# Differential attention on halves of the array's rows, with the second map read against the first half's minimum

## The reference, cut to what matters

```python
def diff_attention(q, k, v, lam, slopes):
    # q, k: (B,S,H,2,Dh), v: (B,S,H,2Dh); S = 2048, H = 4, Dh = 64
    def block(args):                       # 128 queries at a time
        qblk, qp = args
        s = jnp.einsum('bqhce,bkhce->bchqk', qblk, k).astype(jnp.float32) * Dh ** -0.5
        dist = jnp.abs(qp[:, None] - pos[None, :]).astype(jnp.float32)
        s = s - slopes[:, None, None] * dist
        a = jax.nn.softmax(s, axis=-1)
        w = a[:, 0] - lam * a[:, 1]
        return jnp.einsum('bhqk,bkhe->bqhe', w.astype(v.dtype), v)
    ...
a = diff_attention(dq, dk, dv, lam, diff_slopes)
a = rms_norm(a, diff_sub_norm_g[i]) * (1.0 - lam_init)
```

## Time and profile before

| what | value |
|---|---|
| time, median of 3 runs | 2989.01 us (2987.17 to 2992.03) |
| the profiled execution | 2989.96 us, its span 2988.1 us |
| TensorE, weight loads | busy 2801.3 us (94%), 2324.2 us (78%) |
| VectorE, ScalarE, GpSimd | busy 2049.3 (69%), 1554.8 (52%), 1027.6 us (34%) |
| granted TensorE clock, mean | 0.971 |
| the stage of the change | 762 to 1343 us of the span |

### The profile page before, as it was taken

One profiled execution on the slowest core, in us unless ns is written; L12 is line 12 of the kernel. 1 busy time (PEld: TensorE's weight loads), 2 busy tenths in 40 slices (PEclk: granted clock), 3 DMA queues, 4 the chain that ended last, 5 costly groups with the idle time before them and its releaser, 6 DMA issues. The chain is left out here.

```text
span 2988.1 us, 50265 instructions
## 1 busy us (share of the span) xinstructions
PE 2801.3 (94%) x19042; PEld 2324.2 (78%) x19042; DVE 2049.3 (69%) x3063; ACT 1554.8 (52%) x3111; POOL 1027.6 (34%) x736
## 2 busy tenths in 40 slices
PE   6899989999799999998999699899898999799998
PEld 5678867888588888888999578688777778677776
DVE  5766686665888888876777677433567777466675
ACT  6574446643677777766777322322343343355553
POOL 4667657766311111009652444200020111131121
PEclk9999999999899999999999899999999999899999
DMA  3433223333302120004443656342155456654441
GB/s 113 127 106 106 92 85 92 100 105 104 97 23 51 27 54 23 22 11 144 116 117 96 212 198 248 134 143 79 57 161 128 114 142 167 158 165 138 133 154 73
DMA packets 317421, 329.86 MB, mean 110 GB/s; under 512 B 24400, under 2 KB 259968, under 8 KB 314112
## 3 DMA queue, kind: packets, MB, share of 16 engines
q1 hardware_dynamic: 287184, 292.59, 32.1%
q0 software_dynamic: 6912, 23.07, 2.6%
q10 hardware_dynamic: 23088, 11.02, 1.6%
HBM read 217.13 MB, written 109.47 MB: 109 GB/s over the span
## 5 line engine op out<-in xcount | busy, mean ns | idle before, releaser
L1049 PE MATMUL p_acc<-p_y_hi,p_x_hi 128*128 128x512 f32 x904 | 361.7, 400 | 11.6 <-POOL p_x_lo L562 3.8
L1926 DVE CUSTOM_DVE_ANT_0 d_e<-d_score,d_dist,d_slope 128x1024 f32<-128x1024 f32 x256 | 318.5, 1281 | 59.4 <-PE d_score L1988 59.4
L1049 PE MATMUL p_acc<-p_y_lo,p_x_hi 128*128 128x512 f32 x904 | 355.9, 394 | 0.0
L1049 PE MATMUL p_acc<-p_y_hi,p_x_lo 128*128 128x512 f32 x904 | 355.6, 393 | 0.0
L562 POOL TENSOR_TENSOR p_x_lo<-k_carry,p_x_hi 128x1024 fp32r<-128x1024 f32 x113 | 281.1, 2494 | 130.7 <-ACT p_x_hi L634 130.7
L1853 ACT ACTIVATE d_e<-d_e,d_neg_top 128x2048 f32<-128x2048 f32 x128 | 257.0, 2008 | 81.7 <-DVE d_neg_top L1935 81.7
L920 DVE RECIPROCAL p_aux<-p_aux 128x512 f32<-128x512 f32 x64 | 215.1, 3361 | 57.8 <-ACT p_aux L730 57.8
L2011 PE MATMUL d_out<-d_v,d_w_t 128*128 128x128 f32 x2048 | 249.3, 275 | 0.0
L1565 PE MATMUL s_acc<-s_y_hi,s_x_hi 128*128 128x512 f32 x560 | 225.1, 402 | 23.8 <-DVE s_x_lo L1369 13.5
L2011 PEld LDWEIGHTS d_out<-d_v,d_w_t 128*128 128x128 f32 x2048 | 238.6, 192 | 0.0
L1565 PE MATMUL s_acc<-s_y_lo,s_x_hi 128*128 128x512 f32 x560 | 221.9, 396 | 0.0
(11 more groups left out here) (363 smaller groups left out, 6964.0 us busy)
## 6 DMA issues: line engine op xcount, KB each, us to landing
k_carry<-in_w_in SPq DMA_DIRECT2D x128, 256.0 KB, 3.3
k_carry<-in_a_w_in POOLq DMA_DIRECT2D x72, 256.0 KB, 3.6
cols<-p_z SPq DMA_DIRECT2D x64, 256.0 KB, 2.6
w_q<-q SPq DMA_DIRECT2D x15, 1024.0 KB, 8.0
o_parts<-l_stage SPq DMA_DIRECT2D x192, 66.0 KB, 1.8
m_o<-o_parts SPq DMA_DIRECT2D x48, 264.0 KB, 5.9
k_carry<-cols SPq DMA_DIRECT2D x48, 256.0 KB, 4.6
j_x_second<-x SPq DMA_DIRECT2D x20, 512.0 KB, 3.7
```

The lines of the kernel that those rows point to most:

```text
L1049: mm = pe.matmul(bank_of(n, j), x_part[:, n % RING, j, kt], y_part[:, y_slot(n), kt], start=(kt == 0 and m == 0 and not (g == 0 and n % 2 ...
L1926: dve.tensor_tensor_reduce(e[:, m % 3, s, half * HALF:(half + 1) * HALF], score[:, 2 * half:2 * half + 2].rearrange("p a b -> p (a b)"), d ...
```

## The change

`EARLY` is 3; `wait_mixed` waits for the half of the mix that belongs to the group, `wait_turn_free` for `moved` at 4m + 2 group, `wait_group_moved` at 4m + 2 group + 2. The transposes are made in two groups of eight key tiles. Each tile is turned by two instructions, one for the queries 0 to 63 and one for 64 to 127, each on 64 rows and each into its own bank of `turn`; so the two banks are full after one group. The values are two matmuls a tile, one for the keys on rows 0 to 63 and one for the others, into two banks of `out`, which are no longer doubled by unit. ScalarE copies both banks into `a_parts`, GpSimd adds them into `a_out`, ScalarE squares from there, and SyncE's store waits for the add. VectorE's second read of a map takes the first's minimum as its start and yields the whole map's; the reductions of L1935 are gone, and the signs are turned (minimum, exponential of the negative). `mix` has two halves, the first between the reads of the two maps, each of which releases one group of transposes. The orders of work on TensorE, ScalarE and VectorE change, and on GpSimd the adds come between the q and k parts, with `fill` in 8 pieces after the adds at t = 11, 12, 15 of each head.

```diff
             def exp(m, s):
                 h, t = m // NT, m % NT
-                act.wait_ge(top_made, 2 * m + s + 1)
+                act.wait_ge(score_read[1], 2 * m + s + 1)
...
             def move(m, r):
-                act.wait_ge(turned, 4 * m + r + 1)
+                group, side = r // 2, r % 2
+                act.wait_ge(turned, 2 * m + group + 1)
                 if m >= 2 and r == 0:
                     act.wait_ge(valued, m - 1)
-                act.activation(w_t[:, m % 2, 4 * r:4 * r + 4], turn[:, r % 2].rearrange("p (b n) -> p b n", n=P),
-                               ACT.Copy).then_inc(moved, 1)
+                act.activation(w_t[:, m % 2, 8 * group:8 * group + 8, side * HD:(side + 1) * HD],
+                               turn[:, side].rearrange("p (b n) -> p b n", n=HD), ACT.Copy).then_inc(moved, 1)
+            def copy_out(m):
+                act.wait_ge(valued, m + 1)
+                if m >= 2:
+                    act.wait_ge(a_added, m - 1)
+                act.activation(a_parts[:, m % 2], out[:, :, 0:VW], ACT.Copy).then_inc(a_copied, 1)
...
             for m in range(-2, UNITS + 2):
+                if m >= 2:
+                    copy_out(m - 2)
+                if 0 <= m - 1 < UNITS:
+                    move(m - 1, 2)
+                    move(m - 1, 3)
                 if 0 <= m < UNITS:
                     move(m, 0)
                     move(m, 1)
                 if m + 2 < UNITS:
                     exp(m + 2, 0)
                 if m >= 2:
-                    move_out(m - 2)
-                if 0 <= m < UNITS:
-                    move(m, 2)
-                    move(m, 3)
+                    square_out(m - 2)
                 if m + 2 < UNITS:
                     exp(m + 2, 1)
...
+                if half == 0:
+                    bound, least = -LOWEST, half_top[:, m % 2, s:s + 1]
+                else:
+                    dve.wait_ge(score_read[0], 2 * m + s + 1)
+                    bound, least = half_top[:, m % 2, s:s + 1], neg_top[:, m % 2, s:s + 1]
+                dve.tensor_tensor_reduce(
+                    e[:, m % 3, s, half * HALF:(half + 1) * HALF],
+                    score[:, 2 * half:2 * half + 2].rearrange("p a b -> p (a b)"),
+                    dist[:, at:at + HALF], 2.0 ** (-2 * (h + 1)), bound, ALU.add, ALU.min,
+                    least).then_inc(score_read[half], 1)
...
+            for m in range(-2, UNITS):
+                if m + 2 < UNITS:
+                    bias_and_top(m + 2, 0, 0)
...
+                if 0 <= m + 1 < UNITS:
                     invert_total(m + 1)
                 if m + 2 < UNITS:
+                    bias_and_top(m + 2, 0, 1)
+                if 0 <= m + 1 < UNITS:
                     weigh(m + 1)
+                    mix(m + 1, 0)
                 if m + 2 < UNITS:
+                    bias_and_top(m + 2, 1, 0)
+                    bias_and_top(m + 2, 1, 1)
...
+                if 0 <= m + 1 < UNITS:
+                    mix(m + 1, 1)
...
+            def transposes(m, group):
+                wait_mixed(pe, m, group)
+                wait_turn_free(pe, m, group)
+                for b in range(8):
+                    kt = 8 * group + b
+                    for side in range(2):
+                        at = slice(side * HD, (side + 1) * HD)
+                        mm = pe.transpose(turn[:, side, b * HD:(b + 1) * HD], e[at, m % 3, 0, kt * P:(kt + 1) * P],
+                                          ident[at, at])
                 mm.then_inc(turned, 1)
...
+                    if m >= 1:
+                        pe.wait_ge(a_copied, m)
+                    wait_group_moved(pe, m, 0)
                 for kt in range(first, last):
+                    if kt == 8:
+                        wait_group_moved(pe, m, 1)
+                    for side in range(2):
+                        at = slice(side * HD, (side + 1) * HD)
+                        mm = pe.matmul(out[:, side, 0:VW], w_t[at, m % 2, kt], v[at, h % 2, kt], start=(kt == 0),
+                                       stop=(kt == NT - 1))
...
                 if m + 2 < UNITS:
                     scores(m + 2, 0, 0)
                     scores(m + 2, 0, 1)
+                if m >= 1:
+                    values(m - 1, 0, EARLY)
                 if 0 <= m < UNITS:
                     transposes(m, 0)
-                    transposes(m, 1)
-                if m >= 1:
-                    values(m - 1, 0, 7)
                 if m + 2 < UNITS:
                     scores(m + 2, 1, 0)
                     scores(m + 2, 1, 1)
+                if m >= 1:
+                    values(m - 1, EARLY, NT)
                 if 0 <= m < UNITS:
-                    transposes(m, 2)
-                    transposes(m, 3)
-                if m >= 1:
-                    values(m - 1, 7, NT)
+                    transposes(m, 1)
```

More of the change, by code:

```diff
@@ L1652, in fold_distance, with fill @@
                                  op0=ALU.mult, op1=ALU.min).then_inc(self.counted, 1)
-    def fill(self, pool, ident):
+    def fill(self, pool, ident, piece):
         near, tables, own, slopes = self.near[:, 0], self.tables, self.own, self.slopes
[L1657 to L1665, removed]
-            at = slice(side * HD, (side + 1) * HD)
[L1667 to L1677, removed]
@@ new lines, in fill @@
+        if piece == 0:
+            pool.wait_ge(self.counted, 2)
+            for n, (base, step, channel) in enumerate(((P + REACH, -1, 1), (REACH - P, 1, -1))):
+                pool.affine_select(out=near, in_=near, compare_op=ALU.is_ge, fill=MASKED, base=base,
+                                   pattern=[[step, self.WIDE]], channel_multiplier=channel).then_inc(self.counted, 1)
+                pool.wait_ge(self.counted, 3 + n)
+        elif piece == 1:
+            pool.memset(own[:, :].bitcast(F32), 0.0).then_inc(self.made, 1)
+            pool.memset(slopes[:, :].bitcast(F32), 0.0).then_inc(self.made, 1)
+            pool.wait_ge(self.made, 2)
+        elif piece < 6:
+            side, half = (piece - 2) // 2, (piece - 2) % 2
+            at = slice(side * HD, (side + 1) * HD)
+            first = REACH - (half - side) * HD
+            pool.tensor_copy(tables[at, half], near[at, first:first + 2 * P].unsqueeze(1).to_broadcast([HD, 4, 2 * P]))\
+                .then_inc(self.made, 1)
+            for to in (0, 3):
+                pool.tensor_copy(own[at, half, to], near[at, first + REACH:first + REACH + P]).then_inc(self.made, 1)
+            pool.wait_ge(self.made, 3 * piece - 1)
+        else:
+            if piece == 6:
+                pool.wait_ge(self.made, 14)
+                pool.memset(tables[:, :, 0, 0:REACH].bitcast(F32), MASKED).then_inc(self.made, 1)
+                pool.memset(tables[:, :, 3, 2 * P - REACH:2 * P].bitcast(F32), MASKED).then_inc(self.made, 1)
+                pool.wait_ge(self.made, 16)
+            side = piece - 6
@@ L1826, in _ @@
             bias.count_off(pool)
[L1827 to L1832, removed]
+            make_q_hi(1)
+            make_q_lo(1)
+            for m in range(UNITS):
+                h, t, n = m // NT, m % NT, (m + 7) // 4
+                add_out(m)
+                if m % 4 == 1 and n < DIFF_HEADS * QUADS:
+                    make_q_hi(n)
+                    make_q_lo(n)
+                if h + 1 < DIFF_HEADS:
+                    if t == 4:
+                        make_k_hi(h + 1)
+                    if t in (7, 8):
+                        make_k_lo(h + 1, t - 7)
+                    if t in FILLED_AT and 3 * h + FILLED_AT.index(t) < bias.PIECES:
+                        pool.wait_ge(a_added, m + 1)
+                        bias.fill(pool, ident, 3 * h + FILLED_AT.index(t))
         @block.scalar
@@ L1914, in _, with bias_and_top @@
             dve.wait_ge(dist_made, 1)
-            dve.wait_ge(slope_set, DIFF_HEADS)
-            def bias_and_top(m, s):
+            def bias_and_top(m, s, half):
                 h, t = m // NT, m % NT
[L1919 to L1936, removed]
+                if m >= 3 and s == 0 and half == 0:
+                    dve.wait_ge(turned, 2 * (m - 2))
+                if m >= 2:
+                    dve.wait_ge(exped, 2 * (m - 1))
+                dve.wait_ge(scored, 4 * m + 2 * s + half + 1)
@@ new lines, in bias_and_top @@
+                at = S - P - t * P + half * HALF
+                if half == 0:
+                    bound, least = -LOWEST, half_top[:, m % 2, s:s + 1]
+                else:
+                    dve.wait_ge(score_read[0], 2 * m + s + 1)
[5 more added lines that the diff above has]
+                    least).then_inc(score_read[half], 1)
@@ L1945, in weigh @@
                 dve.tensor_scalar(ratio[:, m % 2, 1:2], a_sums[:, h, t:t + 1], ratio[:, m % 2, 0:1], lam[:, 5:6],
[L1946 to L1954, removed]
+                                  ALU.mult, ALU.mult).then_inc(weighed, 1)
@@ new lines, in mix @@
+            def mix(m, half):
+                dve.wait_ge(weighed, m + 1)
```

(10 more changed lines are left out.)

87 lines of the change are left out of this document (39 added, 48 removed).

## The result

The changed kernel takes 3000.68 us (median of 7 runs, 2996.34 to 3002.28), the kernel before 2988.76 us (also 7): ratio 1.0038, 95% interval 1.0027 to 1.0050. It is some 12 us slower, outside the range and on the other side of the forecast. The time lies near that of the first rival (3003), but its mechanism is not what happened, as the rows show.

What follows compares the result with a forecast made beforehand. The prediction took TensorE's order of work (8.79 us a unit) to bound the kernel, and afterwards a ring of waits (8.32): 0.47 over 61 units, 29 us less, median 2960 us, range 2936 to 2982.

Steps and rivals of the forecast that it cites:

- the first rival: Weight loads and streams on TensorE take turns within a half: 0.165 a value pair, time 3003; chance 0.10.
- the one on ScalarE, GpSimd and the queues: ScalarE's chain of 6.5 us, GpSimd's add and q and k parts stay hidden: all at 0, but once at the end.
- the ring: Chain of waits over two units through ScalarE, TensorE and VectorE: 16.64 us, so 8.32 a unit against 8.79 before.
- Transposes at 0.030 an entry: On TensorE, 64x128 transposes cost 0.060 a pair, so both groups take 0.96 us a unit for 1.86.
- Values "nothing gained": On TensorE, 32 value pairs on row halves cost 0.1175 each, 3.75 us a unit, the same as before.
- Border costs gone: On TensorE, switching between 64 and 128 rows stops costing; one half's scores take 0.70; if it stayed, 0.4 a unit returns.
- Carried minimum at no price: On VectorE, bound and slope changing places in the reads costs 0, bounded by 0.15 a read.
- Its wait of 0.17 in the second map: VectorE's second read starts 1.395 after the first (1.205 + 0.08 + 0.11), mostly covered in the first map, not the second.
- the rule for it in the Trainium skill: On TensorE, a weight load overlaps running matmuls only when it is for another group of rows; it spoke against the forecast.
- the exception that the same page makes in its "Step-by-step": A background buffer, named as the exception for TensorE's weight loads; 256-column pairs at 0.12 left the rule no room.
- VectorE alone: Rival: the ring has 0.9 us of unseen slack, so VectorE's chain sets the unit at 7.88, time 2933; chance 0.10.

Runs made afterwards that it cites:

- experiment 1: Changed kernel with GpSimd's waits on the mix put back before its low q parts, k parts and next-stage table pieces: 2965.09 us, ratio 0.9914.
- experiment 3: Changed kernel without new waits, GpSimd making q parts for quads 2 to 15 and k parts for heads 2 and 3 on one column: 2969.60 us, ratio 0.9927.
- experiment 6: Kernel of experiment 1 with one mix of 2048 columns after all four reads in place of two halves: 2942.61 us, ratio 0.9852.

## Why the prediction was wrong

**The step that failed** is the one on ScalarE, GpSimd and the queues: that GpSimd's q and k parts and the add lie hidden, "all at 0". They are hidden as far as their results go; nobody waits for q or k. But VectorE's mix can't run beside them. The trace of before gave two signs. The first: its mixes are all near 2.34, and GpSimd's parts, which wait for `mixed`, run during reads; this part of q starts 0.16 behind the end of the mix that its code waits for, though the profile puts the wait down to a score (timelines of VectorE and GpSimd):

```profile
1025.87 2.34 DVE L1950 SCALAR_TENSOR_TENSOR d_e<-d_e,d_ratio 128x2048 f32<-128x2048 f32 x1
```

```profile
1028.37 1.04 POOL L1806 CAST d_q_hi<-k_carry 128x1024 fp32r<-128x1024 f32 x1 [31.62 <-PE d_score L1988]
```

The second, at the stage's start, where GpSimd fills the next stage's tables with nothing to keep it off the mix: two small copies beside a mix take 2.67, the same two beside reads 0.54.

```profile
780.71 2.34 DVE L1950 SCALAR_TENSOR_TENSOR d_e<-d_e,d_ratio 128x2048 f32<-128x2048 f32 x1
```

```profile
780.54 2.67 POOL L1672 CAST b_own<-b_near 64x128 fp32r<-64x128 f32 x2
...
784.14 0.54 POOL L1672 CAST b_own<-b_near 64x128 fp32r<-64x128 f32 x2
```

There GpSimd is the one that stands until the mix is over: in these rows, the engine whose instruction comes second waits. The diff removes three waits on the mix, and I priced the work that was moved, not what these waits had kept apart. That is the term put at nothing; it measured 26.7 us of stalls. The Trainium skill (GPSIMD Engine Reference, "8. Key points") says that GpSimd shares its SBUF interfaces with VectorE, with contention when the VectorE instruction has two SBUF inputs. This trace agrees and gives the size: the mix doesn't slow down but stands until GpSimd's instruction is over (end of the mix 1.09 after it), while the reads, with one input in PSUM, keep 1.28.

**How 26.7 us of stalls become 37 us.** The stall holds the second exponential, the copy behind it and TensorE's values; the ring has no slack for 1.3 to 2.2 us. Then the granted clock falls: the nine stretches at 0.83 and 0.91 lose 14 us of clock together. 26.7 and 14 are 41, an estimate from above, as a part of it lies in the 0.4 of slack that VectorE has a unit. That the clock falls because of the stalls is shown in so far as it stays at 1.00 in experiments 1 and 3; how much of the 37 us is its own share was not measured apart.

**The ring was right.** Its legs in experiment 1, on TensorE and then on VectorE:

```profile
1205.32 0.94 PE L2067 MATMUL d_out<-d_v,d_w_t 64*128 64x128 f32 x12 [0.69 <-ACT d_a_parts L1912]
1206.39 0.71 PE L2050 MATMUL d_turn<-k_ident,d_e 64*128 64x64 f32 x16
1206.88 0.51 PE L2039 MATMUL d_score<-d_k_hi,d_q_hi 64*128 64x512 f32 x2
...
1208.35 3.09 PE L2067 MATMUL d_out<-d_v,d_w_t 64*128 64x128 f32 x52
1211.25 0.69 PE L2050 MATMUL d_turn<-k_ident,d_e 64*128 64x64 f32 x16
1211.72 0.51 PE L2039 MATMUL d_score<-d_k_hi,d_q_hi 64*128 64x512 f32 x2
...
1214.44 0.72 PE L2050 MATMUL d_turn<-k_ident,d_e 64*128 64x64 f32 x16
...
1223.21 0.71 PE L2050 MATMUL d_turn<-k_ident,d_e 64*128 64x64 f32 x16
```

```profile
1212.87 1.23 DVE L1977 CUSTOM_DVE_ANT_0 d_e<-d_score,d_dist 128x1024 f32<-128x1024 f32 x1 [0.76 <-PE d_score L2039]
...
1214.28 1.28 DVE L1977 CUSTOM_DVE_ANT_0 d_e<-d_score,d_dist,d_half_top 128x1024 f32<-128x1024 f32 x1
...
1215.79 1.28 DVE L1998 SCALAR_TENSOR_TENSOR d_e<-d_e,d_ratio 128x1024 f32<-128x1024 f32 x1
1217.00 1.22 DVE L1977 CUSTOM_DVE_ANT_0 d_e<-d_score,d_dist 128x1024 f32<-128x1024 f32 x1
...
1218.39 1.28 DVE L1977 CUSTOM_DVE_ANT_0 d_e<-d_score,d_dist,d_half_top 128x1024 f32<-128x1024 f32 x1 [0.17 <-ACT d_e L1897]
```

From transposes to transposes it is 8.05 and 8.77, 16.82 for two units, where the prediction had 16.64. From the end of VectorE's last read (1218.39 + 1.28) over ScalarE to the first transposes (1223.21) it is 3.54 (forecast 3.47); transposes, scores and values from 1206.39 to 1211.72 take 5.33 (forecast 0.48 + 1.39 + 3.05 + 0.48 = 5.40); the first score to the read 1.15 (1.00); VectorE from 1212.87 to the end of the last read 6.80 (6.77). So 8.41 a unit against 8.32, and 26 us against 29.

**By points.** Transposes at 0.030 an entry: right. Values "nothing gained": 0.112 a pair, a little better than 0.1175. Border costs gone: right only in part. The last score pair hands over to the values after 0.23, but the first pair behind the transposes takes 0.31, so the scores of one half take 1.47 (1206.88 to 1208.35), where the prediction had 1.39 and the kernel before 1.59; the row of the next stage that it went by shows the 0.48 of the transposes and not the length of the score pair behind them. That the TensorE leg still came out near is luck in this one point: the cheaper values (2.90 for 3.05) cover it. Carried minimum at no price: right for the second read; the first, with constants alone, became shorter, 1.22. Its wait of 0.17 in the second map as forecast. The first rival (loads and streams in turn) is refuted by 0.112; the rule for it in the Trainium skill (TensorE: Matmul & The Clock Gate, Part 3) does not hold for these pairs, and they agree with the exception that the same page makes in its "Step-by-step". "VectorE alone" was wrong for this version, though the whole mix (8.06) comes within 0.4 us of its own VectorE chain (7.65). The rival that decided was not among those named.

## What to carry to other kernels

When a diff removes a wait that guards no data, ask what it kept apart in time, and look at the other engine's instruction lengths beside it: a maximum near the median is evidence of a schedule, not of independence. Place GpSimd's long instructions in VectorE's reads from PSUM, and cut them so that each fits (2.41 us beside two reads of together 2.6 here). And when an engine stands on a ring with others, splitting its work to release a consumer earlier is a loss if the consumer can't start then anyway: even the whole mix ends 1.3 us before the transposes start in experiment 6 (1208.20 and 1209.52), and the half before it cost 18 us.

## What was not expected of the hardware

VectorE's instruction with two inputs in SBUF doesn't share with GpSimd but waits for the end of GpSimd's running instruction: a half mix ended 1.07 to 1.09 behind it, whatever its own start, and with a 4.64 us subtraction a mix of 2.34 took 6.6 to 6.8 us. It holds the other way round too: two small copies of GpSimd beside a running mix took 2.67 in place of 0.54. A memset of GpSimd, which reads nothing, did not take part in this, in the one place where it met a half mix in the changed kernel (memset 909.74, 1.06 us; half mix 909.94, 1.28 us). A wait of TensorE of about 1.4 us, after shorter ones in the same unit, was followed by some 3 us at the lower clock level (stretches at 0.83), but not every time (eight of the 14 long mixes on q), while 0.7 us in every second unit was not (1.00 from 800 to 1300 us in experiment 1).
